# The sums of the modulation's last four rows moved from attention into the projections

## What is computed

```
mod = silu(c) @ w_ada + b_ada            # [6 * 1024]: sh1, sc1, g1, sh2, sc2, g2
h = rms_norm(x, norm1_w) * (1 + sc1) + sh1
q, k, v, f_logit, gb, gc, u = split(h @ w_in)
attn = forgetting_attention(rms_norm(q), rms_norm(k), v, log_sigmoid(f_logit + b_forget))
conv = gb * causal_short_conv(gc * u)    # width 3
x = x + g1 * (concat(rms_norm(attn), rms_norm(conv)) @ w_out)
x = x + g2 * moe_ffn(rms_norm(x) * (1 + sc2) + sh2)   # 32 experts, 4 per token
```

## Time and profile before

| | us |
|---|---|
| median of 3 runs | 2389.22 |
| the profiled execution's own time | 2392.84 |
| its span in the trace | 2391.2 |
| TensorE busy | 2255.1 |
| VectorE busy | 1742.3 |
| ScalarE busy | 1293.0 |
| GpSimd busy | 794.3 |
| first matmul of attention | 392.48 |
| first work of the mixer | 567.3 |
| first work of the experts' stage | 726.9 |

### The profile page before, as it was taken

One profiled execution on the slowest core, in us unless ns is written; L12 is line 12 of the kernel. 1 busy time (PEld: TensorE's weight loads), 2 busy tenths in 40 slices (PEclk: granted clock), 3 DMA queues, 4 the chain that ended last, 5 costly groups with the idle time before them and its releaser, 6 DMA issues.

```text
span 2391.2 us, 37523 instructions
## 1 busy us (share of the span) xinstructions
PE 2255.1 (94%) x10570; PEld 1819.6 (76%) x10571; DVE 1742.3 (73%) x2124; ACT 1293.0 (54%) x1736; POOL 794.3 (33%) x784
## 2 busy tenths in 40 slices
PE   6899997888976999999999999999999999999997
PEld 2679876776764788888878888878888887878886
DVE  1684423577765799976689866687999768689697
ACT  2332212675324677755567655566777556576575
POOL 2153003792234233432223222232333322233242
PEclk9899998899987999999999999999999999999999
DMA  7134205882235899987689967697999868799695
GB/s 245 61 128 146 59 17 131 249 224 78 106 115 200 288 370 372 372 290 232 215 283 373 361 216 231 224 321 241 368 378 361 302 215 276 261 330 371 230 352 176
DMA packets 299220, 583.98 MB, mean 244 GB/s; under 512 B 23889, under 2 KB 53601, under 8 KB 297057
## 3 DMA queue, kind: packets, MB, share of 16 engines
q1 hardware_dynamic: 269248, 501.68, 60.2%
q0 software_dynamic: 26560, 69.06, 10.6%
q10 hardware_dynamic: 3362, 12.59, 1.4%
HBM read 544.79 MB, written 44.24 MB: 246 GB/s over the span
## 4 chain that ended last, share of the span: by engine, by line
PE 62%; DVE 4%; issue 2%; DVEq 1%; DMA 0%; ACT 0%; ACTq 0%; POOL 0%; POOLq 0%
PE psum L2036 55%; DVE d_wlo L1863 3%; PE psum L2018 3%; PE psum L1976 2%; PE psum L1986 2%; DVE d_up L1876 0%; DMA d_xg<-xn_d,d_entry 0%; DVE d_act L1882 0%; DMA d_entry<-list_d 0%; DVE d_atlo L1888 0%; DVEq L1542 0%; DVE d_y_two L1853 0%; DVEq L1541 0%; ACT d_y_two L1764 0%; DVEq L1540 0%
## 5 line engine op out<-in xcount | busy, mean ns | idle before, releaser
L1863 DVE TENSOR_TENSOR d_wlo<-d_raw,d_whi 128x1024 fp32r<-128x1024 f32 x578 | 673.8, 1218 | 81.5 <-ACT d_whi L1739 79.9
L1739 ACT ACTIVATE d_whi<-d_raw 128x1024 fp32r<-128x1024 f32 x578 | 574.6, 1053 | 117.8 <-PE psum L2036 86.0
L2036 PE MATMUL psum<-d_whi,d_xthi 128*128 128x512 f32 x1152 | 458.7, 398 | 0.1
L2036 PE MATMUL psum<-d_whi,d_xtlo 128*128 128x512 f32 x1152 | 454.6, 395 | 0.0
L2036 PE MATMUL psum<-d_wlo,d_xthi 128*128 128x512 f32 x1152 | 454.5, 394 | 0.0
L1863 DVE TENSOR_TENSOR d_wlo<-slab,d_whi 128x1024 fp32r<-128x1024 f32 x292 | 343.5, 1218 | 15.4 <-ACT d_whi L1739 13.6
L1642 POOL DMA_INDIRECT out_dram<-d_yst,d_dest x49 | 93.3, 1905 | 781.5 <-DVE d_yst L1910 724.8
L1739 ACT ACTIVATE d_whi<-slab 128x1024 fp32r<-128x1024 f32 x292 | 292.5, 1054 | 6.0 <-PE psum L2036 5.6
L2036 PEld LDWEIGHTS psum<-d_whi,d_xtlo 128*128 128x128 f32 x1152 | 217.0, 188 | 50.7
L2036 PEld LDWEIGHTS psum<-d_whi,d_xthi 128*128 128x128 f32 x1152 | 217.0, 188 | 50.0 <-issue 1.6
L2036 PEld LDWEIGHTS psum<-d_wlo,d_xthi 128*128 128x128 f32 x1152 | 217.2, 189 | 48.3
(11 more groups left out here) (322 smaller groups left out, 3984.4 us busy)
## 6 DMA issues: line engine op xcount, KB each, us to landing
slab<-in_w_gate_up_dram SPq DMA_DIRECT2D x144, 1024.0 KB
d_raw<-in_w_gate_up_dram SPq DMA_DIRECT2D x144, 1024.0 KB, 9.0
d_raw<-in_w_down_dram SPq DMA_DIRECT2D x144, 1024.0 KB, 7.1
b_wp<-in_w_ada_dram POOLq DMA_DIRECT2D x16, 1024.0 KB, 7.7
slab<-in_w_in_dram SPq DMA_DIRECT2D x12, 1024.0 KB, 5.5
slab<-in_w_ada_dram SPq DMA_DIRECT2D x8, 1024.0 KB
a_xin<-in_x_dram ACTq DMA_DIRECT2D x2, 2048.0 KB
v_d<-a_vst POOLq DMA_DIRECT2D x16, 256.0 KB, 2.7
```

What stands on the lines that cost most here:

```text
L1739: nc.scalar.activation(whi[n % NW][:, part, :], raw[n % NRAW][:, part, :], ACT.Copy).then_inc(whi_ok, 1)
L1863: nc.vector.tensor_tensor(wlo[n % NW][:, part, :], raw[n % NRAW][:, part, :], whi[n % NW][:, part, :].bitcast(F32), ALU.subtract).then_inc ...
L2036: mm = nc.tensor.matmul(to, m_[:, KH * h + k, :], w_[n % NW][:, k, :], start=(h == 0 and k == 0 and q == 0), stop=(h == 1 and k == KH - 1 ...
```

## The change

The sum moves from attention_block to project_block, and GpSimd does all of it. It now comes in 32 pieces of 128x1024: piece r is row block r % 8 of row r // 8. The two buffers are wp, made of the two halves of qraw and of stage, which are free after the last store of q and k. modacc is taken from the right side of SBUF, over the place of the x that has been turned by then. To make room, further tiles share places: nolist (the list of empty entries stored at the start) lies in qhi, fz and fa in h32, cum in sq, chi in qhi, clo in qlo; ScalarE waits for nolist's store before it first writes qhi. The small memsets of pone, mone and ucv come ahead of the v stores. Attention loses its GpSimd loop, ScalarE's scalings and b_wp. Its remaining GpSimd work is two memsets.

`release` is gone, with its three clears and barriers. `retire(nc, 0)` clears the first stage's semaphores on GpSimd at the start of the mixer, with no barrier.

In GpSimd's program the pieces stand so: multiply and add of pieces 0 to 7 alternate with the 16 v stores; 8 to 11 after them; then the wait for chi and clo and the eight stores; 12 to 18; the multiply or add of 19 and 20 behind each of the first four squares; 21 to 31 before the memset of the early tile and the fifth square.

```diff
-    def release(self, nc):
-        nc.clear_and_free_semaphores(self.held)
-        nc.all_engine_barrier()
+    def retire(self, nc, stage):
+        nc.clear_and_free_semaphores(self.stages[stage])
...
+                    if NQK - 6 <= k < NQK - 2:
+                        pool.wait_ge(hT_mm, 2 * KT)
+                        own.link(nc.gpsimd.memset(s.modacc[:, (k - NQK + 6) * D:(k - NQK + 7) * D], 0.0))
+                    if k == NQK - 2:
+                        pool.dma_start(s.modacc[0:1, :], a["b_ada"][0:1, 2 * D:6 * D]).then_inc(bada_in, 16)
...
+                def fetch(r):
+                    k, at = r % KT, 2 * D + r // KT * D
+                    pool.dma_start(wp[r % 2][:, :], a["w_ada"][0, k * P:(k + 1) * P, at:at + D]).then_inc(wp_in[r % 2], 16)
+
+                def scale(r):
+                    pool.wait_ge(wp_in[r % 2], 16 * (r // 2 + 1))
+                    own.link(nc.gpsimd.tensor_tensor(wp[r % 2][:, :], wp[r % 2][:, :],
+                                                     s.csilu[:, r % KT:r % KT + 1].broadcast_to([P, D]), ALU.mult))
+
+                def add(r):
+                    cols = slice(r // KT * D, (r // KT + 1) * D)
+                    own.link(nc.gpsimd.tensor_tensor(s.modacc[:, cols], s.modacc[:, cols], wp[r % 2][:, :], ALU.add))
+                    if r + 2 < 4 * KT:
+                        fetch(r + 2)
+
+                pool.wait_ge(bada_in, 16)
+                for r in range(2):
+                    fetch(r)
                 for m, n in enumerate(v_units):
...
+                    if m % 2:
+                        add(m // 2)
+                    else:
+                        scale(m // 2)
+                for r in range(KT, KT + 4):
+                    scale(r)
+                    add(r)
                 pool.wait_ge(ext_ok, 2)
...
+                for r in range(KT + 4, 2 * KT + 3):
+                    scale(r)
+                    add(r)
                 for k in range(2 * CT):
                     ct, h = k // 2, k % 2
                     if k == 2 * CT - 4:
+                        for r in range(2 * KT + 5, 4 * KT):
+                            scale(r)
+                            add(r)
                         pool.wait_ge(unit_mm, last_unit[len(slabs) - 2] + 1)
...
+                    if k in (0, 2):
+                        scale(2 * KT + 3 + k // 2)
+                    if k in (1, 3):
+                        add(2 * KT + 3 + k // 2)
...
-                    for r, at in scaled_at.items():
-                        if c in (at, at + 1):
-                            half = slice((c - at) * (PW // 2), (c - at + 1) * (PW // 2))
-                            act.wait_ge(wp_in[r % 2], 16 * (r // 2 + 1))
-                            nc.scalar.activation(wp[r % 2][:, half], wp[r % 2][:, half], ACT.Copy,
-                                                 scale=s.csilu[:, r % KT:r % KT + 1]).then_inc(scaled_ok, 1)
```

More of the change, by code:

```diff
@@ L39, in semaphores @@
     def semaphores(self, nc):
-        self.held = []
+        self.stages.append([])
         def sem(name):
-            self.held.append(nc.alloc_semaphore(name=name))
-            return self.held[-1]
+            self.stages[-1].append(nc.alloc_semaphore(name=name))
+            return self.stages[-1][-1]
         self.idle = sem(f"idle{nc.next_id()}")
@@ L169, in project_block @@
         chanmean = sb("a_chanmean", [P, P], F32)
-        nolist = sb("a_nolist", [P, s.E * T // P, 3], I32)
+        nolist = qhi_all[:, 0:3 * s.E * T // P].bitcast(I32).rearrange("p (n c) -> p n c", c=3)
         with ExitStack() as early:
@@ L174, in project_block @@
         ucv = [sb(f"a_ucv{i}", [P, T + 2], F32) for i in range(2)]
-        fz, fa, fe = (sb(f"a_f{i}", [H, HALF], F32) for i in "zae")
-        cum = sb("a_cum", [H, T], F32)
-        chi, clo = sb("a_chi", [H, T], F32R), sb("a_clo", [H, T], F32R)
+        s.modacc = s.until_mixed.enter_context(nc.sbuf_tensor("modacc", [P, 4 * D], F32, side="right"))
+        fz, fa, fe = h32[0][0:H, :], h32[1][0:H, :], sb("a_fe", [H, HALF], F32)
+        cum, chi, clo = sq_all[0:H, :], qhi_all[0:H, :], qlo_all[0:H, :]
         pone, mone = sb("a_pone", [H, T], F32), sb("a_mone", [H, T], F32)
@@ L198, in project_block @@
         dve_own, pool_own = sem("a_dve_own"), sem("a_pool_own")
-        nolist_st = sem("a_nolist_st")
+        nolist_st, bada_in = sem("a_nolist_st"), sem("a_bada_in")
+        wp_in = [sem(f"a_wp_in{i}") for i in range(2)]
         pad_ok, early_in = sem("a_pad_ok"), sem("a_early_in")
@@ L308, in _ @@
                         store_q(pool, k - 2)
+                    if NQK - 6 <= k < NQK - 2:
[3 more added lines that the diff above has]
+                        pool.dma_start(s.modacc[0:1, :], a["b_ada"][0:1, 2 * D:6 * D]).then_inc(bada_in, 16)
                 store_q(pool, NQK - 2)
                 store_q(pool, NQK - 1)
+                own.link(nc.gpsimd.memset(pone[:, :], 1.0))
+                own.link(nc.gpsimd.memset(mone[:, :], -1.0))
+                for i in range(2):
+                    own.link(nc.gpsimd.memset(ucv[i][:, 0:2], 0.0))
+                pool.sem_inc(consts, 1)
+                def fetch(r):
[13 more added lines that the diff above has]
+                    fetch(r)
                 for m, n in enumerate(v_units):
@@ L747, in _ @@
             def _(pool):
-                own = Chain(pool, pool_own)
-                def fetch(r):
-                    k, at = r % KT, 2 * D + r // KT * PW
-                    pool.dma_start(wp[r % 2][:, :], a["w_ada"][0, k * P:(k + 1) * P, at:at + PW]).then_inc(wp_in[r % 2], 16)
-                fetch(0)
                 for n, x in enumerate((q2, k2)):
                     nc.gpsimd.memset(x[1][HD:P, :].bitcast(F32), 0.0).then_inc(pad_ok, 1)
-                    pool.wait_ge(pad_ok, n + 1)
-                own.link(nc.gpsimd.memset(s.modacc[:, :], 0.0))
-                pool.dma_start(s.modacc[0:1, :], a["b_ada"][0:1, 2 * D:6 * D]).then_inc(bada_in, 16)
-                fetch(1)
-                pool.wait_ge(bada_in, 16)
-                for r in range(NPIECE):
-                    cols = slice(r // KT * PW, (r // KT + 1) * PW)
-                    k = r % KT
-                    if r in scaled_at:
-                        pool.wait_ge(scaled_ok, 2 * (list(scaled_at).index(r) + 1))
-                    else:
-                        pool.wait_ge(wp_in[r % 2], 16 * (r // 2 + 1))
-                        own.link(nc.gpsimd.tensor_tensor(wp[r % 2][:, :], wp[r % 2][:, :],
-                                                         s.csilu[:, k:k + 1].broadcast_to([P, PW]), ALU.mult))
-                    own.link(nc.gpsimd.tensor_tensor(s.modacc[:, cols], s.modacc[:, cols], wp[r % 2][:, :], ALU.add))
-                    if r + 2 < NPIECE:
-                        fetch(r + 2)
             @block.scalar
@@ L2085, in build @@
             s.fold = s.sb("fold", [P, s.HD], F32, mixer)
+            s.until_mixed = mixer
             project_block(nc, s, arrays)
[L2087 removed]
             s.attn = s.sb("attn", [P, s.NT, s.DA], F32, mixer)
[L2089 removed]
             s.whi0 = s.sb("whi0", [P, s.KT, s.HALF], F32R, mixer)
             attention_block(nc, s, arrays)
[L2092 removed]
             mixer_block(nc, s, arrays)
[L2094 removed]
         expert_block(nc, s, arrays, out)
```

36 lines of the change are left out of this document (13 added, 23 removed).

## The result

The changed kernel took 2431.23 us, median of 4 runs (2430.93 to 2435.97), beside 2390.36 us (2386.52 to 2394.75) for the kernel before on the same chip: a ratio of 1.0175, 95% interval 1.0162 to 1.0187. That is 40.9 us slower. The prediction said 2418, between 2395 and 2443.

What follows compares the result with a forecast made beforehand. TensorE bounds the kernel; GpSimd's late squares would hold it up in the projections. 28 + 10 + 2.8 - 0.85 - 13 - 1.5 + 3 = +28.5 us on the median 2389.22 gives 2418, eight in ten from 2395 to 2443.

Steps and rivals of the forecast that it cites:

- rival C: Projections: GpSimd and VectorE shut each other out fully, GpSimd losing 20 to 25 us; +51, 2440 us; chance 0.20.
- one of the signs that the prediction named for being wrong: Wrong if GpSimd idles before the fifth square, the stage ends before 410 us, or attention takes under 150.
- the main line: The likeliest case: GpSimd comes late to the fifth square and TensorE waits; +28.5 us, 2418; chance 0.65.
- Part 1, a piece: Projections: one 128x1024 piece costs GpSimd 1.90 + 0.08 + 2.40 + 0.30 + 0.57 = 5.25 us.
- Part 1, the sum: Before the fifth square: 170.7 us wanted, 142.3 free; GpSimd 28 us late, waits at v units, first and fifth square included.
- Part 2: Projections: about 50 VectorE operations cost GpSimd 0.22 each, +10 us (0 to 30); room after VectorE's own delay taken as enough.
- Part 3: End of projections: drain of 100 DMAs +2.8 us, clear and barrier gone -0.85; attention's and mixer's ends -1.5 together.
- Part 4: Attention, heads 0 to 2: ScalarE's scalings, waits and reads go, -13 us (-22 to -5); low granted clock at first stays.
- Part 5: Projections' tail: TensorE waits 7 us or more, may run some 14 us at half speed; +3 us (0 to +10).
- The -1.5 for the clears and barriers behind attention and mixer: Ends of attention and mixer: removing clears and barriers saves 1.5 us for both; low bound 0.

Runs made afterwards that it cites:

- y3: Changed kernel with the wait for chi and clo and the eight stores moved behind pieces 12 to 18: 2424.27 us, ratio to before 1.015.
- z2: y3 plus a whole piece, instead of a half, behind each of the first four squares: 2419.04 us, ratio to before 1.0114.
- x2: Changed kernel with GpSimd's multiplies and adds replaced by memsets of about equal time, reading nothing: last square at 427.61 us; only first stages compared.
- x4: Kernel before with one GpSimd drain added behind its eight small stores: 2385.96 us, ratio to before 0.9983.
- z1: Changed kernel with 16 of 32 pieces in the projections, the rest summed by GpSimd in attention, and drains in idle places: 2373.49 us, ratio to before 0.9931.
- x1: Changed kernel without the multiplies and adds of the 32 pieces, fetches kept: last square at 393.96 us; only first stages compared.
- x3: Changed kernel with one more all-engine barrier after each of the first three stages: 2432.3 us.
- y1: Changed kernel with the semaphore clears and barrier back behind each of the first three stages: 2436.07 us, ratio to before 1.0194.
- y2: Kernel before with ScalarE's four scaled pieces in attention scaled on GpSimd instead: 2382.84 us, ratio to before 0.9967.

## Why the prediction held, and where its sum was short

**Place and direction** were right: GpSimd has too little room before the fifth square, TensorE waits there for its squares, the drain grows, attention gives back a part. Time and range held, 2431 in 2395 to 2443, but 13 us over the forecast and 9 under rival C. And one of the signs that the prediction named for being wrong did show: GpSimd idles before the fifth square. So the account of GpSimd in the main line didn't hold, and the range did in part because it had been drawn wide enough for rival C.

**Part 1, a piece.** 5.25 us forecast. Measured 1.91 and 2.41, 0.08 and 0.30 between, 0.57 to 0.60: 5.3. Straight lines between rows of 512 and 2048 columns were good to 1%.

**Part 1, the sum: the step that failed** is the sentence "with GpSimd as the bound the three waits are no separate costs, they sum to 28". It takes for granted that GpSimd is never kept waiting once it is late. The fifth square was to come at 365.98 + 28.4 + 10 = 404.4 and came at 423.6, 19.2 later. Of these, 7.95 are the wait for chi and clo, 8.0 those ahead of the first, third and fourth square (1.12 + 3.25 + 3.63), 1.0 a late landing of the last piece but one, 0.8 a later start of v's units, which other profiles show without any edit, some 1.8 the pauses of 0.30 ahead of v's stores that were counted per pair of units but not in the sum; part 2 was 1.8 too high, which goes off; the rest, 1.4, is about what 32 pieces dearer by 0.04 make. When pace changes hands along a chain (ScalarE's v tile, then VectorE's logits, then TensorE's units between two squares, each released by the engine that was late), each stretch costs its own maximum, and the maxima add up to more than GpSimd's total. How the 8.0 and 7.95 split over these releases wasn't tried one by one. y3 and z2 took 11.4 us off the last square by order alone, where 16 us of idle had been. Fifth to last square then took 17.0 us instead of 18.8 + 3, which gives 4.9 back: 14.3 short in this stage.

**Part 2.** 10 us forecast for GpSimd's loss. 17 of 32 adds were stretched, by 8.2 us in sum; multiplies weren't (1.89 to 1.96). That is right in size, but the engine that pays is VectorE: taps of 1285 ns took 3304, 60 us more busy time in all. The sentence "The room after VectorE's own delay I take as enough in the likeliest case" failed here: its delay is what GpSimd waited for at chi and clo. This much of rival C is true (a slab's split of 11 us and a wait of 5 forecast, 9.56 and 7.95 found), while its 20 to 25 us of loss on GpSimd isn't. The Trainium skill's page "SBUF — State Buffer", section "Who interferes with whom", says that the port pair the two engines share is an exclusive lock, so the loser blocks until the other is done. For VectorE the trace agrees: a tap grew by 2.0 us, the length of one multiply (1.91) or most of an add (2.41), and with writes alone on GpSimd (x2) the tap grew by nothing. For GpSimd the stretch of 0.3 to 0.9 us is under a whole tap's 1.3.

**Part 3.** Drain +2.8 forecast; 8929 against 6239 ns is +2.7. From last square to first matmul +1.9 (forecast 2.8 - 0.85 = 1.95). x4 and z1 confirm the reading that it goes by DMAs.

**Part 4.** -13 forecast, -15.2 found. The first 249 matmuls, heads 0 and 1, took 66.3 us before; in after:

```profile
450.05:502.00 51.95, 47.06 (x249) 40.04 (x249) 33.04 (x58) 31.05 (x75) 1.84 (x2) 0.81 0.66 164
502.00:609.00 107.00, 93.55 (x617) 79.39 (x615) 75.96 (x143) 73.88 (x175) 0.00 (x0) 1.00 0.35 86
```

So 14.3 of the 15.2 are there, where the prediction put them, and the rest of the stage is unchanged at the full granted clock (108.0 before). The granted clock of these first heads stayed low, 0.81, as forecast, behind a pause of TensorE of 7.36 us (7.4 forecast). In x1, x3, y1, y3 and z2, which do the same work in attention, it was 0.96 to 0.97 over the stage, 0.89 to 0.91 in the first 52 us, and the stage took 156 to 157 us. After, with 0.94 and 159.6, was at the slow end: TensorE was at a mean of 0.74 from 460 to 480 us, in x3 at 1.00. So what attention gives back is 15 to 19 us, and part 4 was too small by 2 to 6.

**Part 5.** +3 forecast, for a wait of 7 us and some 14 us at half speed. TensorE stood still for 13.1 us, from 411.6 to 424.7. The granted clock was 1.2 GHz from 417 to 428.5, and 2.4 GHz from 429 on, so only 4 us of work ran at half speed. The fifth square's product and the unit behind it took 8.4 us, the next product and unit 6.3: 2.1 us.

**The rest.** Mixer +2.8 and experts -2.0 weren't forecast. The experts' difference is within what identical code showed (1662.0 to 1664.3 us from GpSimd's first work in before, x4 and y2); the mixer's stays open, as said under y1. The -1.5 for the clears and barriers behind attention and mixer can't be read in a total: y1 went 4.8 us the expected way, with an interval as wide.

## What to carry to other kernels

An engine that is idle 75% of a stage has room only between fixed points: lay its new work against each stretch between two waits, and add the excess of every stretch, not the total against the total. Idle time spent beside VectorE is cheap while nobody waits for VectorE and dear once its slowed chain reaches the engine that slowed it. Before moving work to save a stage, take away the one part that was on its path: here one line (ScalarE's scalings) and three drains in idle places gave 17 us, and the sums' place nothing that could be measured. And two traces are compared by distances from a common point behind which the edits begin: here absolute times differed by up to 4 us without any edit.

## What the runs showed of the hardware

A drain of GpSimd's queue took 0.083 us for each DMA issued there since the last (67, 17, 32 and 100 DMAs: 5.6, 1.44, 2.67, 8.2 us behind the last work), although the stage had waited for their landing; at the kernel's end it took 4.9 us. A drain set in idle time ahead brought the closing one to 0.21 to 0.76 us. Behind 24 indirect stores in the mixer of z1 a middle drain ended 2.6 us after the last of them.

GpSimd and VectorE slow each other unevenly: the price fell on VectorE (+2.0 us on a 1.3 us tap) and hardly on GpSimd's adds (0.3 to 0.9 on 2.4). GpSimd's writes alone left VectorE's operations on two tiles of SBUF as they were (taps 1284 ns, splits 2.5 us). Not so one operation on a single tile: the TENSOR_SCALAR a_h<-a_h of 8x512 took 0.41 us before and without sums (x1), 2.51 in after, and 0.80 and 1.26 beside writes alone (x2).
